# Four edits to a two-block network: gate tiles, the norm between the layers, gathered squares, moved splits

## The reference

```python
# first block, layer i
n = rmsnorm(h, norm_g[i])
z = n @ w_in[i] + b_in[i]              # 25 tiles of 128 features here; the last two are the pool's gate
...                                     # causal convolution of 31 taps, pooling, attention, each times silu(gate)
h = h + concat(ya, yb, yc) @ w_out[i]
h = h + (p[i] @ ple_w[i]) * sigmoid(h @ ple_gate_w[i])
# second block, layer l
mod = silu(c) @ w_ada[l] + b_ada[l]     # six rows: shift, scale and gate, twice
u  = modulate(rmsnorm(x, g), sh1, sc1) @ w_in[l]       # and the same of the context xc
x  = x + g1 * (mixer(u) @ w_out[l])
h  = modulate(rmsnorm(x, g), sh2, sc2)
x  = x + g2 * (conv_ffn(h) @ w_down[l])                # the context too, but not in the last layer
out = rmsnorm(x, g_final)
```

## Time and profile before

| | |
|---|---|
| time, median of 3 runs | 1448.06 us (1447.2 to 1451.13) |
| the profiled execution: time, span | 1448.6 us, 1446.7 us |
| mean granted TensorE clock | 0.983 |
| TensorE busy | 1381.4 us, 95% |
| VectorE busy | 1043.0 us, 72% |
| ScalarE busy | 708.0 us, 49% |
| GpSimd busy | 48.0 us, 3% |
| data moved | 151 GB/s on average |

### The profile page before, as it was taken

One profiled execution on the slowest core, in us unless ns is written; L12 is line 12 of the kernel. 1 busy time (PEld: TensorE's weight loads), 2 busy tenths in 40 slices (PEclk: granted clock), 3 DMA queues, 4 the chain that ended last, 5 costly groups with the idle time before them and its releaser, 6 DMA issues.

```text
span 1446.7 us, 21853 instructions
## 1 busy us (share of the span) xinstructions
PE 1381.4 (95%) x8475; PEld 1188.1 (82%) x8475; DVE 1043.0 (72%) x1993; ACT 708.0 (49%) x1191; POOL 48.0 (3%) x67
## 2 busy tenths in 40 slices
PE   6999999999999999898999999999899988899997
PEld 5788987879978786577888888888788867899997
DVE  6597786978779886737789998676544755788854
ACT  5537666366544642734444434312335635666643
POOL 0000000000000012000000000000000210000000
PEclk9999999999999999998999999999899999999999
DMA  7643556325376531031454455577233331455552
GB/s 261 221 148 118 171 178 220 131 89 189 128 258 224 160 103 45 16 117 55 136 168 152 160 166 164 186 266 253 99 113 105 116 103 58 131 191 176 185 186 96
DMA packets 61943, 218.52 MB, mean 151 GB/s; under 512 B 7024, under 2 KB 9072, under 8 KB 61456
## 3 DMA queue, kind: packets, MB, share of 16 engines
q1 hardware_dynamic: 59200, 205.55, 43.1%
q0 software_dynamic: 2496, 11.56, 2.3%
q10 hardware_dynamic: 144, 0.00, 0.0%
HBM read 216.04 MB, written 1.05 MB: 150 GB/s over the span
## 4 chain that ended last, share of the span: by engine, by line
PE 80%; DVE 8%; ACT 7%; issue 2%; DMA 2%; DVEq 0%; ACTq 0%
PE bank L574 19%; PE bank L576 19%; PE bank L575 19%; PE bank L590 5%; DVE DP L1957 2%; ACT WHI L1325 2%; PE bank L1149 1%; DVE WLO L1864 1%; DMA RAWB<-in_ws 1%; ACT L1325 1%; PE bank L635 1%; PE bank L636 1%; PE bank L637 1%; PE bank L612 1%; PE bank L613 1%
## 5 line engine op out<-in xcount | busy, mean ns | idle before, releaser
L574 PE MATMUL bank<-NHI,WHI 128*128 128x256 f32 (+1 forms) x1392 | 463.4, 333 | 8.3 <-DVE WLO L1864 7.0
L1864 DVE TENSOR_TENSOR WLO<-RAWB,WHI 128x1024 fp32r<-128x1024 f32 (+1 forms) x276 | 328.4, 1192 | 192.5 <-ACT WHI L1325 191.6
L576 PE MATMUL bank<-NHI,WLO 128*128 128x256 f32 (+1 forms) x1392 | 457.5, 329 | 0.0
L575 PE MATMUL bank<-NLO,WHI 128*128 128x256 f32 (+1 forms) x1392 | 457.4, 329 | 0.0
L1325 ACT ACTIVATE WHI<-RAWB 128x1024 fp32r<-128x1024 f32 (+1 forms) x276 | 283.2, 1029 | 204.8 <-PE bank L576 117.0
L574 PEld LDWEIGHTS bank<-NHI,WHI 128*128 128x128 f32 x1392 | 264.3, 190 | 42.9 <-issue 10.2
L575 PEld LDWEIGHTS bank<-NLO,WHI 128*128 128x128 f32 x1392 | 264.4, 190 | 24.4 <-issue 1.4
L576 PEld LDWEIGHTS bank<-NHI,WLO 128*128 128x128 f32 x1392 | 264.4, 190 | 23.7
L1957 DVE CUSTOM_DVE_ANT_0 DP<-RAWB,CREP,PRM 128x1024 f32<-128x1024 f32 x120 | 153.9, 1282 | 7.8 <-DMA RAWB<-in_ws 2.2
L1325 ACT ACTIVATE CF<-bank,PRM 128x512 f32<-128x512 f32 (+1 forms) x88 | 59.1, 672 | 177.5 <-PE bank L576 174.8
L574 PE MATMUL bank<-HHI,WHI 128*128 128x512 f32 (+1 forms) x352 | 119.1, 338 | 0.0
(11 more groups left out here) (326 smaller groups left out, 1905.6 us busy)
## 6 DMA issues: line engine op xcount, KB each, us to landing
RAWB<-in_ws SPq DMA_DIRECT2D x364, 512.0 KB, 3.4
RAWB<-in_ws SPq DMA_DIRECT2D x32, 384.0 KB, 3.7
NB<-in_nab POOLq DMA_DIRECT2D x12, 256.0 KB, 3.3
CREP<-in_crep POOLq DMA_DIRECT2D x2, 1024.0 KB, 6.6
K<-in_c POOLq DMA_DIRECT2D x2, 896.0 KB, 5.7
K<-in_c POOLq DMA_DIRECT2D x1, 1344.0 KB, 8.0
X<-in_xt SPq DMA_DIRECT2D x4, 256.0 KB, 5.1
X<-in_xt POOLq DMA_DIRECT2D x1, 1024.0 KB, 6.8
```

Of the source, the lines that this page charges most:

```text
L574: nc.tensor.matmul(o, hi[:, w], xh, start=(i == 0), stop=False)
L575: nc.tensor.matmul(o, hi[:, w], xl, start=False, stop=False)
L576: ins = nc.tensor.matmul(o, lo[:, w], xh, start=False, stop=(i == slabs - 1))
L1864: V.tensor_tensor(WLO[:, k % SPL, 0:w], RAWB[:, u % RAW, 0:w], WHI[:, k % SPL, 0:w].bitcast(F32), ALU.subtract).then_inc(S("lo_ready"), 1)
```

## The change

1. **Gate tiles.** The last two of the 25 tiles (23 and 24) of each layer of the first block go through `fm` on split weights; the native ones are 13 to 22. ScalarE and VectorE split four more units in all.
2. **Norm between the layers by halves.** The last down tile is made for the latents first, then for the context into bank 6. Residual, square, sums (`half_sums`, banks 4 and 5), root, and spread are made for each half by itself; slabs go in the order HALF_ORDER: latent slabs 0 to 5, context slabs 0 to 5, latent 6 and 7, context 6 and 7. The values follow by halves, with the units 0 to 2 used twice. The latents' scaled slabs go to CF instead of TB2. The splits stand at the places (-1, 2, 4, 13) of this order.
3. **Squares in one slab.** In every `stats_behind` VectorE adds gathered slab 0, gathered slab 1 and the last but one square into one slab (two adds more), and TensorE sums two slabs instead of four. The norms concerned are those behind both mixers and both down products of the second block.
4. **Moved steps.** ScalarE makes the silu of c before slab 7 of the first norm. The split in front of the first values of the second block goes from slab 4 to slab 6 on both engines.

The diff, cut, its indentation eight columns less; `pair_by_halves`, which nothing calls, is left out.

```diff
-NATIVE_FROM = Z1["kb"]
+NATIVE_TILES = range(Z1["kb"], NZ1 - 2)
...
+HALF_ORDER = [(s, c) for c in range(2) for s in range(KS - 2)] + [(s, c) for c in range(2) for s in (KS - 2, KS - 1)]
...
-    add([UNIT], t >= NATIVE_FROM)
+    add([UNIT], t in NATIVE_TILES)
...
+def scaled_half(s, c, beside_hidden):
+    if beside_hidden and c == 0:
+        return CF[:].rearrange("p w k t -> p (w k t)")[:, s * T:(s + 1) * T]
+    return TB2[:, s, c * T:(c + 1) * T]
...
+    def half_sums(c, sq):
+        b, last = 4 + c, sq.shape[1] - 1
...
+        if c == 0:
+            pe.wait_ge(S("sq_gathered"), me.nth("sq_gathered"))
+            me.nth("sq_ready", KS // 2)
+        pe.wait_ge(S("sq_ready"), me.nth("sq_ready"))
+        for k in (0, last):
+            for t in range(TT):
...
+        ins.then_inc(S("ms_ready"), 1)
...
+    def half_spread(c):
...
+        pe.wait_ge(S("r_tok"), me.nth("r_tok"))
...
+        for t in range(TT):
+            ins = nc.tensor.transpose(bank[b][:, t * P:(t + 1) * P],
+                                      GR[:, 3, TT * c + t:TT * c + t + 1].broadcast_to([P, P]), cst("ident"))
+        ins.then_inc(S("r_spread"), 1)
+        if c == 1:
+            held[4] = held[5] = (S("t_ready"), me.nth("t_ready", 2 * KS))
+    def last_tile_by_halves(slabs, rhs, sq, spread_at):
+        units, b0 = [], me.next_tile()
+        for c in range(2):
...
+            if b in held:
...
+            o = bank[b][:, 0:T]
+            for s in range(slabs):
+                if c == 0 and s % 8 == 0:
+                    units.append(unit())
+                if c == 1 and s == 5:
+                    half_sums(0, sq)
+                if c == 1 and s == spread_at:
+                    half_spread(0)
...
+                xh, xl = (x[:, c * T:(c + 1) * T] for x in rhs(s))
+                nc.tensor.matmul(o, hi[:, w], xh, start=(s == 0), stop=False)
+                nc.tensor.matmul(o, hi[:, w], xl, start=False, stop=False)
+                ins = nc.tensor.matmul(o, lo[:, w], xh, start=False, stop=(s == slabs - 1))
+                if c == 1 and s % 8 == 7 and s != slabs - 1:
+                    ins.then_inc(S("unit_done"), 1)
+            ins.then_inc(S("lat_made" if c == 0 else "unit_done"), 1)
...
+    def values_by_halves():
+        def part(u, c, done, between=None):
+            hi, lo = units[u]
+            given = ("l_split", "x_split")[c]
+            for i in range(4):
+                k, t = (i // 2, 2 * c + i % 2) if u < 3 else (i % 2, 2 * c + i // 2)
+                s, cols = 2 * u + k, slice(k * VW, (k + 1) * VW)
...
+                if i in (0, 2) and u < 3 or i < 2 and u == 3:
+                    pe.wait_ge(S(given), me.nth(given))
...
+            if done:
+                ins.then_inc(S("unit_done"), 1)
+        units = {}
+        for u in range(3):
+            units[u] = unit()
+            part(u, 0, False, (lambda: half_spread(1)) if u == 2 else None)
+            if u == 0:
+                half_sums(1, SQF)
+        for u in range(3):
+            part(u, 1, True)
+        units[3] = unit()
+        part(3, 0, False)
+        part(3, 1, True)
+        for b in range(4):
...
-        nt, last = n // P, sq.shape[1] - 2
...
+        nt, last = n // P, sq.shape[1] - 1
+        for k in (0, last):
...
+                pe.wait_ge(S("sq_gathered"), me.nth("sq_gathered"))
+            else:
...
+                pe.wait_ge(S("sq_ready"), me.nth("sq_ready"))
             for t in range(nt):
                 ins = nc.tensor.matmul(bank[4][:, 0:nt], sq[:, k, t * P:(t + 1) * P], PICK[:, NTOK - 1 - t:NTOK - 1 - t + nt],
-                                       start=(first and t == 0), stop=(end and t == nt - 1))
-            return ins
...
-        slab(0, True, False)
-        slab(1, False, False)
-        me.nth("sq_ready", KS // 2 - 1)
-        pe.wait_ge(S("sq_ready"), me.nth("sq_ready"))
-        slab(last, False, False)
-        pe.wait_ge(S("sq_ready"), me.nth("sq_ready"))
-        slab(last + 1, False, True).then_inc(S("ms_ready"), 1)
+                                       start=(k == 0 and t == 0), stop=(k == last and t == nt - 1))
+        ins.then_inc(S("ms_ready"), 1)
...
-            elif t < NATIVE_FROM:
+            elif t in NATIVE_TILES:
+                native(b, "z_freed")
+            else:
...
-            else:
-                native(b, "z_freed")
...
-            spread_scales("r_tok", "r_spread", NTOK)
-            held[4] = (S("t_ready"), me.nth("t_ready", 2 * KS))
-            tm(4, VW, "x_split")
+            values_by_halves()
...
-        for m in range(KS):
+        for m in range(KS - 1 if uc else KS):
             fm(FT, n, lambda s: (HHI[:, s, 0:n], HLO[:, s, 0:n]), "wo_freed", "hid_split" if m == 0 else None)
-            stats_behind(m, n, SQF)
+        if uc:
+            last_tile_by_halves(FT, lambda s: (HHI[:, s, :], HLO[:, s, :]), SQF, 12)
+        else:
+            stats_behind(KS - 1, n, SQF)
...
-    def residual(n, units, sq):
+    def shift_by_halves(l, shift, beside_hidden, sq, sq_at, root_at, rests, split_at=None):
+        guess(GR[:, 0, 0:TT], GR[:, 2, 0:TT], "ms_eps")
+        if -1 in rests:
+            rest()
+        for i, (s, c) in enumerate(HALF_ORDER):
+            if i == sq_at:
+                act.wait_ge(S("wo_freed"), me.nth("wo_freed"))
+                A(sq[:, sq.shape[1] - 1, T:TC], X[:, KS - 1, T:TC], ACT.Square).then_inc(S("sq_ready"), 1)
+            if i in rests:
+                rest()
+            if i == split_at:
+                split_to(me.u + 1 + AHEAD)
+            if i == root_at:
+                guess(GR[:, 0, TT:], GR[:, 2, TT:], "ms_eps")
+            act.wait_ge(S("t_ready"), me.nth("t_ready"))
+            A(NHI[:, s, c * T:(c + 1) * T], scaled_half(s, c, beside_hidden), ACT.Identity,
+              bias=MOD[:, l, shift + s, c:c + 1]).then_inc(S("xh_ready"), 1)
+    def residual(n, units, sq, halves=False):
...
+            if halves and m == KS + 1:
+                act.wait_ge(S("wo_lat"), me.nth("wo_lat"))
+                A(sq[:, ring - 1, 0:T], X[:, KS - 1, 0:T], ACT.Square).then_inc(S("sq_ready"), 1)
+                continue
...
-                rest(units)
+                rest(1 if halves and m == KS - 1 else units)
...
                 rest()
+            if l == 0 and s == 7:
+                act.wait_ge(S("ld_prm"), 16)
+                act.wait_ge(S("cv_zeroed"), 1)
+                A(CV2[:, :, 8:10], prm_col("cvec", 0, 2 * KS).rearrange("p (s c) -> p s c", c=2), ACT.Silu).then_inc(S("c_ready"), 1)
...
-        if l == 0:
-            act.wait_ge(S("ld_prm"), 16)
...
-            if l == 0 and t == 1:
-                act.wait_ge(S("cv_zeroed"), 1)
-                A(CV2[:, :, 8:10], prm_col("cvec", 0, 2 * KS).rearrange("p (s c) -> p s c", c=2), ACT.Silu).then_inc(S("c_ready"), 1)
...
-            guess(GR[:, 0, :], GR[:, 2, :], "ms_eps")
-            shift_hi(l, TC, SH1, (2, 5))
+            shift_by_halves(l, SH1, True, SQF, 3, 4, (-1, 2, 4, 13))
...
-                if s == 4:
+                if s == 6:
...
-        residual(n, 3, SQF)
+        residual(n, 3, SQF, uc)
...
-    def rsqrt(m, g, t, out, done="dve_chain"):
+    def rsqrt(m, g, t, out, done="dve_chain", beside=None):
...
             V.scalar_tensor_tensor(t, m, -0.5, g, ALU.mult, ALU.mult).then_inc(S("dve_chain"), 1)
+            if beside is not None:
+                beside(o is out)
...
         if m == KS - 1:
-            me.nth("sq_used")
-            me.nth("sq_ready", 2)
+            dve.wait_ge(S("sq_used"), me.nth("sq_used"))
+            V.tensor_tensor(sq[:, 0, 0:n], sq[:, 0, 0:n], sq[:, 1, 0:n], ALU.add).then_inc(S("dve_chain"), 1)
+            dve.wait_ge(S("dve_chain"), me.nth("dve_chain"))
+            dve.wait_ge(S("sq_ready"), me.nth("sq_ready"))
+            V.tensor_tensor(sq[:, 0, 0:n], sq[:, 0, 0:n], sq[:, sq.shape[1] - 2, 0:n], ALU.add).then_inc(S("sq_gathered"), 1)
...
-        if s == 4:
+        if s == 6:
...
+    def last_residual(l, gate):
+        dve.wait_ge(S("unit_done"), tile_end[0])
+        V.scalar_tensor_tensor(X[:, KS - 1, T:TC], bank[6][:, 0:T], MOD[:, l, gate + KS - 1, 1:2], X[:, KS - 1, T:TC],
+                               ALU.mult, ALU.add).then_inc(S("wo_freed"), 1)
...
+    def modulate_by_halves(l, gain, shift, scale, before, beside_hidden, residual_at, root_at, rests, split_at=None):
+        V.scalar_tensor_tensor(GM[:], MOD[:, l, scale:scale + KS, :], 1.0, bl(prm_col(gain, 0, KS), 2),
+                               ALU.add, ALU.mult).then_inc(S("dve_chain"), 1)
...
+        me.nth("sq_ready")
+        def root(c, beside=None):
+            g = slice(TT * c, TT * (c + 1))
+            dve.wait_ge(S("ms_ready"), me.nth("ms_ready"))
+            V.tensor_scalar(GR[:, 0, g], bank[4 + c][:, 0:TT], EPS, None, ALU.add).then_inc(S("ms_eps"), 1)
+            rsqrt(*(GR[:, i, g] for i in (0, 2, 1, 3)), "r_tok", beside)
+        def scaled(i):
+            s, c = HALF_ORDER[i]
```

(57 more changed lines are left out.)

58 lines of the change are left out of this document (55 added, 3 removed).

## The result

| | before | changed |
|---|---|---|
| median of 9 runs | 1450.2 us (1447.08 to 1455.64) | 1440.53 us (1437.9 to 1447.18) |
| the profiled execution: time, span | 1448.6 us, 1446.7 us | 1446.7 us, 1444.9 us |
| mean granted TensorE clock | 0.983 | 0.980 |

The ratio is 0.9938, 95% interval 0.992 to 0.9955: 9 us faster, 6.5 to 11.6. Two more series of the changed kernel on other chips gave 0.9942 (0.992 to 0.9964) and 0.9934 (0.9908 to 0.996). The forecast was 8.1 us less.

The account below looks back on a forecast made before the run. It took TensorE, busy 95% of the span and carrying 80% of the chain, as the bound. Terms 5.3 + 1.0 - 0.7 + 1.4 + 1.1 + 0 = 8.1 us off 1448.6 gave 1440.5, range 1437.0 to 1445.0 (8 in 10).

Parts of the forecast that it names:

- norm by halves: Norm between the layers: next tile starts at 1058.2 instead of 1063.45, gain 5.3 us, bounds 2.4 and 6.5.
- squares, first mixer: First layer's norm, 512 columns: sums lose half their matmuls, guess comes earlier, gain 1.0 us, bounds 0 and 1.0.
- squares, second mixer: Second layer's norm, 256 columns: two adds ahead of VectorE's residual delay the guess, loss 0.7 us, bounds 0.2 and 0.9.
- silu: Silu of c moved before slab 7: TensorE's 2.13 us wait before the row products goes, gain 1.4 us, bounds 0.5 and 2.1.
- split at slab 6: Second block's first values: later split shortens TensorE's 1.73 us wait at 396.32, gain 1.1 us, bounds 0.5 and 1.7.
- gate tiles: Split weights save TensorE 3.2 us, which becomes idle time because ScalarE is the path; gain 0.
- so the low clock costs 2.8 us: Norm between the layers, 1043 to 1049: 19 matmuls took 6 us, but would take 3.2 at full clock.
- rival 1: TensorE's clock still falls after 1038 in the halved norm, so 2.8 us are lost: 1443.3 us; chance 14%.
- The forecast of the clock itself: Norm between the layers: TensorE's granted clock was to stand at 1.0 from 1034 to 1056.
- one of the signs that were to speak against the forecast: TensorE waiting for SQF or SQ, the buffers of squares, would show the forecast wrong.
- Rival 4: Silu and second-block split bring 0.5 us each, since raw loads come next: 1442.0 us, or 1443.0; chance 10%.
- rival 2: Gate tiles pay because the path runs through TensorE, so 3.2 us more come out: 1437.3 us; chance 13%.

Follow-up runs that it names:

- e2: Changed kernel with the norm between the layers made whole again; ratio to the kernel before 0.9979 (0.9961 to 0.9996).
- e4: Kernel before with 14 idle matmuls ahead of the transposes of the norm between the layers and 18 behind; ratio to the kernel before 1.0007.
- e11: Changed kernel run unaltered, for the third time; ratio to the kernel before 0.9934 (0.9908 to 0.996).
- e6: Changed kernel with the last two gate tiles native again; ratio to the kernel before 0.9925 (0.9908 to 0.9942).
- e1: Changed kernel run again unaltered; ratio to the kernel before 0.9942 (0.992 to 0.9964).
- e3: Changed kernel with the silu of c back behind the second latent tile; ratio to the kernel before 0.9943 (0.9923 to 0.9964).

## Why the prediction was right, and where it was not

The time, 1440.53 for a forecast of 1440.5, is nearer than the terms deserve, and that is luck: the forecast took 8.1 us from 1448.6, while the kernel before came out at 1450.2 and the gain at 9.0 us, 9.7 by the medians. Term by term, with the steps of the table (positive is a gain):

| part | forecast | measured |
|---|---|---|
| norm by halves | 5.3 (2.4 to 6.5) | 5.92 to 5.95 in ten profiles; 5.4 by time (e2) |
| squares, first mixer | 1.0 (0 to 1.0) | 0.92 or 0.93 in seven profiles, 0.39 to 0.71 in four (step from 640 to 664) |
| squares, second mixer | -0.7 (-0.9 to -0.2) | -0.71 in five profiles, -0.82 and -0.87 in two |
| silu | 1.4 (0.5 to 2.1) | about 1.0 (0 to 1.4) |
| split at slab 6 | 1.1 (0.5 to 1.7) | 0.9 at the place |
| gate tiles | 0 | 0.0 in both layers |
| sum | 8.1 | 7.5 to 8.0 by these places; 9.0 (6.5 to 11.6) by time |

**The norm.** The working held closely. In the time of the kernel before (1.91 us less than the trace's) the context half was to end at 1035.6 and ended at 1035.4, the values at 1056.3 and ended at 1056.4, and the next tile was to come at 1058.2 and came at 1057.5: the copies out of the banks overlap more than I gave them. e2's 0.42 for the gathered slab is in the 5.9; the halves alone are 5.5. What they bring can be split: VectorE's first low part comes 8.65 us sooner (1035.26 - 1.91 against 1042.00), and from there to the next tile it takes 24.15 in place of 21.45 us, 2.70 more, because slabs wait for the second root and for splits.

**The low clock.** The step that failed is "so the low clock costs 2.8 us". It had TensorE's own matmuls priced at two speeds and left out that VectorE sets the pace of the values at either; e4 shows 21.46 us with all of it at the full clock, e2 21.48 with the clock low for the first 4.15, and the kernel before 21.45 with it low for the first 6.77. (The 1.14 us between 1038 and 1043 that it counts as value work are the four transposes.) So rival 1's price had no ground; what a low clock would cost in the halved norm, where TensorE has 48 matmuls in 6 us beside the context half, no run shows. It was no term of the sum, which is why the forecast survived. The argument against rival 1 was weak too: it says that the level fell only where TensorE had 1.14 us of work in 5, but the clock of the kernel before also fell at 202, 574, 663, 1188 and 1243. The forecast of the clock itself was right: it stayed at 1.00 there in all ten profiles with the halved norm. The Trainium skill ("TensorE: Matmul & The Clock Gate", A second HAM failure mode) speaks of short idles between groups that make the clock go up and down; the halved norm, with waits up to 1.1 us, does not show it in any run. What three profiles of the changed kernel show at 440 is another thing, one fall at one wait of 1.6 to 2.8 us.

**Squares.** The second mixer was right to the digit: two adds ahead of the residual, seen at 0.45 us each, 0.71 on the path. TensorE's wait of 1.21 us for the gathered slab is one of the signs that were to speak against the forecast; the table load covers it, so the sign was badly chosen. At the first mixer it depends on where the clock falls. In the first profile it falls at 664.30, amid the second half of the sums, which takes 1.53 us and not 0.9, and the guess stands 1.87 us behind the start of the table load where it stood 2.31: 0.44 of the 1.0 came. In e11 it falls at 664.14, just behind the sums, and the guess stands 1.40 us behind: 0.91. Timelines of ScalarE in the first profile, then in e11:

```profile
663.86 1.28 ACT L1450 ACT_TABLE_LOAD   x1
665.73 0.20 ACT L1450 ACTIVATE GR<-GR 128x4 f32<-128x4 f32 x1 [0.58 <-DVE GR L2058]
```

```profile
662.95 1.28 ACT L1450 ACT_TABLE_LOAD   x1
664.35 0.20 ACT L1450 ACTIVATE GR<-GR 128x4 f32<-128x4 f32 x1
```

The distance is 1.39 or 1.40 us in seven of the eleven profiles with the new sums, and 1.61 to 1.92 in the other four. So the term was right where the clock holds through the sums, and had no part for the case where it does not.

**Silu.** Right in kind, a third too large. The raw loads behind it were named as next, with 0.5 as the price if they came at once; the table has executions on either side of that. What it did not have is that TensorE itself would stand for one of these loads, 0.3 to 1.7 us. The Trainium skill ("ScalarE: Activation LUTs", What ACT_TABLE_LOAD costs) adds a drain of 1.38 us to a load; in its new place the load starts 0.02 us behind the split, the silu starts 1.29 us after the load's start, and the copy that follows is on time:

```profile
30.39 1.05 ACT L1450 ACTIVATE WHI<-RAWB 128x1024 fp32r<-128x1024 f32 x1
31.46 1.28 ACT L1450 ACT_TABLE_LOAD   x1
32.75 0.22 ACT L1450 ACTIVATE CV<-PRM 128x16 f32<-128x16 f32 x1
33.13 0.42 ACT L1450 ACTIVATE NHI<-Y 128x256 fp32r<-128x256 f32 x1 [0.15 <-DVE Y L2169]
```

With a drain of 1.38 us the silu would have ended at 34.35 and the copy at 33.13 would have come 1.2 us later, an estimate from the Trainium skill's figure ("ScalarE: Activation LUTs", What ACT_TABLE_LOAD costs); the trace doesn't agree.

**Split.** 0.9 us at the place where 1.1 was forecast, by the way that was forecast: TensorE's wait shrinks from 1.73 to 0.27 us, and it then waits 0.45 for the low part of the first tile. Rival 4 (the raw load comes next) is partly right too: 30 us later VectorE waits 1.98 us for one.

**Gate tiles.** 0, for the reason given: ScalarE's row of work keeps its 10.06 us, and TensorE's saving turned into two waits. TensorE's idle time at the taps was forecast at 0.3 us and is 0.37. Its saving was put at 0.8 us a tile and is 0.6, so rival 2's price of 3.2 us was too high.

**What the sum left out.** It had no term for what an earlier TensorE runs into later. By 439 the changed kernel is 3.1 to 3.5 us ahead, and in all three profiles it gives back 2.7 to 4.4 of these at the next point where it depends on VectorE and the loads. Two more places take time from profiles of the changed kernel: 2.4 us between 560 and 600 in all three, and 1.7 between 1180 and 1185 in two, where the clock falls at 1176.30 and 1174.87 behind a wait of 1.91 us that every profile has. In the times the gain is there all the same, 8.4 to 9.6 us.

## What to carry to other kernels

A stretch at half the TensorE clock costs only what the engine that sets its pace lets it cost: before pricing it, measure from that engine's first instruction to the end of the stretch in an execution where the clock was high. An edit that removes a wait hands the time to the next resource in line, here the raw loads, so look for the next wait on each engine 10 to 50 us downstream. And where single terms are smaller than the scatter of the times, match the instructions of two traces in order and read the steps of their distance, since two profiled executions of the same kernel can stand several us apart.

## What the hardware showed

Two profiles of the same code ahead of 30 us differ by up to 1.4 us, mostly by when the clock first rises, between 12.2 and 15.1 us from the start of the span. It falls in different executions at different places: at 440 in nine of the thirteen profiles, behind waits of TensorE of 0.69 to 2.77 us, but not in e6 behind a wait of 1.33 us, nor in the kernel before behind one of 0.80, while e4, the same code there, has it behind 1.22. Near 1175 every profile has a wait of 1.91 us, and the clock falls behind it in three of the thirteen (the first, e1 and e3); at 202 it falls in four, near 595 in eight. In e4 the clock fell during the 32 small matmuls of the sums and stayed low through 14 full matmuls of 256 columns without a gap.
